# A transformer block on eight cores: first stage pipelined by x slab, a norm row loaded earlier, the MLP output's norm split, the sigmoid from Exp and Ln

## Reference

```python
hn = rms_norm(h, g_pre_mix)
u, q, k, v, f_logit = split(hn @ w_in)          # f_logit + b_f
y_pool = multiscale_pool(u, w_pool, pool_scale)
y_attn = forgetting_attention(q, k, v, log_sigmoid(f_logit))
y = concat(rms_norm(y_pool, g_pool_out), rms_norm(y_attn, g_attn_out)) @ w_out
h = h + rms_norm(y, g_post_mix)
a = relu(rms_norm(h, g_pre_mlp) @ w_up)
h = h + rms_norm((a * a) @ w_down, g_post_mlp)
gate = sigmoid(rms_norm(h, g_ple_gate) @ w_gate)
h = h + rms_norm(gate * (p @ w_ple), g_post_ple)
```

## Time and profile before

| what | us |
|---|---|
| median of 6 runs | 1717.58 |
| lowest and highest | 1696.63, 1854.65 |
| the profiled execution | 1719.45 |
| its span on core 4, the slowest | 1718.3 |
| TensorE busy in the span | 1615.6 (94%) |
| VectorE, ACT, GpSimd busy | 558.9, 504.4, 121.4 |
| read from and written to HBM | 252.16 MB, 25.17 MB |

### The profile page before, as it was taken

How to read it: one execution, slowest core, us unless ns; L and a number is a source line. 1 busy time by engine, 2 the same in 40 slices (tenths; PEclk the granted TensorE clock), 3 DMA queues, 4 the chain that set the end, 5 groups by cost and what they waited for, 6 DMA issues and landing times.

```text
span 1718.3 us, 24144 instructions; the slowest of 8 cores (1691.3 to 1718.3 us)
## 1 busy us (share of the span) xinstructions
PE 1615.6 (94%) x8588; PEld 826.0 (48%) x8700; DVE 558.9 (33%) x915; ACT 504.4 (29%) x1071; POOL 121.4 (7%) x241
## 2 busy tenths in 40 slices
PE   4799999999986999999999999999999999999895
PEld 2457566665553444444444444444444444444342
DVE  3564132222345444212112121212121121465445
ACT  3553444444542443110001100011000111355355
POOL 2002000001000001000000000000000000001000
PEclk9878889999998999999999999999999999999998
DMA  9544121315365448735353534435353536567646
GB/s 238 156 136 74 31 44 26 50 26 88 61 113 109 133 132 182 125 67 93 54 98 52 97 65 83 80 67 93 55 98 51 97 66 139 143 193 190 141 126 217
DMA packets 42308, 175.71 MB, mean 102 GB/s; under 512 B 4688, under 2 KB 4944, under 8 KB 33616
## 3 DMA queue, kind: packets, MB, share of 16 engines
q0 software_dynamic: 31824, 103.20, 36.3%
q1 hardware_dynamic: 10368, 70.96, 12.5%
HBM read 252.16 MB, written 25.17 MB: 161 GB/s over the span
## 4 chain that ended last, share of the span: by engine, by line
PE 82%; DVE 5%; ACT 4%; DMA 4%; issue 4%; DVEq 0%; ACTq 0%; POOL 0%; SPq 0%; POOLq 0%
PE pb L312 81%; DMA grow<-gb 2%; DMA wring_66<-wqkv 1%; ACT junkb L330 1%; PE pb L693 1%; DMA wring_65<-wv 1%; ACT stats L330 1%; ACT L330 0%; DVE accd L340 0%; ACT rstdB L330 0%; DVE m_115 L345 0%; DVE m_111 L345 0%; DVE m_113 L345 0%; DVE m_110 L345 0%; DVE m_114 L345 0%
## 5 line engine op out<-in xcount | busy, mean ns | idle before, releaser
L330 ACT ACTIVATE rt_101<-pb 128x512 f32<-128x512 f32 x64 | 38.2, 597 | 511.0 <-PE pb L312 510.5
L312 PE MATMUL pb<-hT,wslot_104 128*128 128x512 bf16 x512 | 111.3, 379 | 2.0 <-DVE hT L340 2.0
L312 PE MATMUL pb<-wslot_106,hidden 128*128 128x512 bf16 x504 | 111.9, 379 | 0.4
L312 PE MATMUL pb<-wslot_107,hidden 128*128 128x512 bf16 x503 | 111.8, 379 | 0.5
L312 PE MATMUL pb<-wslot_105,hidden 128*128 128x512 bf16 x497 | 110.7, 379 | 0.8
L312 PE MATMUL pb<-hT,wslot_105 128*128 128x512 bf16 x512 | 111.2, 379 | 0.0
L312 PE MATMUL pb<-hT,wslot_106 128*128 128x512 bf16 x512 | 111.2, 379 | 0.0
L312 PE MATMUL pb<-hT,wslot_107 128*128 128x512 bf16 x512 | 111.2, 379 | 0.0
L312 PE MATMUL pb<-wslot_104,hidden 128*128 128x512 bf16 x500 | 109.9, 379 | 0.6
L340 DVE TENSOR_TENSOR hidden<-rt_101 128x512 bf16<-128x512 f32 x64 | 44.3, 692 | 177.9 <-ACT rt_101 L330 177.9
L340 DVE TENSOR_TENSOR hidden<-rt_102 128x512 bf16<-128x512 f32 x64 | 44.3, 692 | 174.1 <-ACT rt_102 L330 174.1
(11 more groups left out here) (310 smaller groups left out, 2356.5 us busy)
## 6 DMA issues: line engine op xcount, KB each, us to landing
wslot_104<-wmlp POOLq DMA_DIRECT2D x32, 512.0 KB, 9.5
wslot_105<-wmlp POOLq DMA_DIRECT2D x32, 512.0 KB, 8.7
wslot_106<-wmlp POOLq DMA_DIRECT2D x32, 512.0 KB, 9.4
wslot_107<-wmlp POOLq DMA_DIRECT2D x32, 512.0 KB, 9.5
xst_59<-xT SPq DMA_DIRECT2D x6, 1024.0 KB, 5.8
xst_60<-xT SPq DMA_DIRECT2D x5, 1024.0 KB, 5.5
xst_61<-xT SPq DMA_DIRECT2D x5, 1024.0 KB, 7.3
xt_95<-xo SPq DMA_DIRECT2D x4, 1024.0 KB, 6.7
```

Source lines behind the costliest of these rows:

```text
L312: pe.op(lambda h: h.matmul(o, lhsT, rhs, start=bool(start), stop=bool(stop), skip_group_check=True), r=(lhsT, rhs), w=(o,), signal=bool(st ...
L330: act.op(lambda h: h.activation(o, i, func, **kw), r=r, w=w)
```

## The change

Four parts.

1. First stage: a slab's casts and squares are emitted ahead of the sums of the slab before, squares in one ACT pass of 2048 columns, sums in two wide adds. The casts of the next block's first slab stand ahead of this block's root, its squares behind all evictions. The queries that were in the first block go elsewhere: none after block 0, 16 after blocks 1 and 2 (eight on each side of the `onesf` matmul), 32 after block 3. SyncE waits before some x loads for quarters of the key weights, and the second query ring (`wring_68`) is issued after the second block.
2. `grow` for the mixer is loaded when the first half of `u` is done (`biasT` lies elsewhere for that); `y_pair` yields twice per tile between scaling and transposing.
3. `norm2` is split: the second half of the add goes to GpSimd (not for tile 7); `norm2h` is the cast; `norm2b`, the squares in two halves with the root and a change of sign, comes a tile later, in the middle of the next tile's `down` calls; the transposes come two tiles later, inside a `down`. The norm of tile 7 is emitted among the first gates.
4. The sigmoid is Exp(-Ln(1 + Exp(-z))), three ACT passes. `wple` is in two pieces, the scale by the last `grow` starts after the first eight gates, two per gate.

```diff
@@ startup
+        def casts(h, sl):
...
+        def squares(h, sl):
+            n = 4 * h + sl
+            actf(sq[n % 2], xst[n % 3], AF.Square)
+            if n == 1:
+                sp.wait(wk_ev[2])
+            xload(n + 3)
...
+        fills = ((), ((0, 0),), ((1, 0),), ((0, 1), (1, 1)))
+        for h, (own, half) in enumerate(halves):
             for sl in range(4):
+                if sl or not h:
+                    casts(h, sl)
+                    squares(h, sl)
+                if sl:
+                    sums(h, sl - 1)
+                project(h, sl)
+            sums(h, 3)
...
+            if fill:
+                query(fill[0][0], fill[0][1], 6, range(0, 8))
+            mm(bank(7), onesf, acc2[:, 0, :], True, True)
+            if h < 3:
+                casts(h + 1, 0)
+            rsqrt(rb, bank(7), float(D))
+            if fill:
+                query(fill[0][0], fill[0][1], 6, range(8, KC))
...
+            if h < 3:
+                squares(h + 1, 0)
+            if h == 1:
+                pool.wait(Ev(act.sem, "act", act.count, "act"))
+                pload(3)
@@ mix_main
         done.add("uA")
+        sp.dma(grow, gb_in[0])
...
         while "att" not in done:
             yield
-        sp.dma(grow, gb_in[0])
@@ y_pair
             v_ts(yb[:, i, 1024:2048], yb[:, i, 1024:2048], col1(r_a, i))
-        yield
+            yield
+            yield
@@ norm2
         v_stt(m[t], m[t], col1(r_m, t), grow, ALU.mult, ALU.mult)
-        v_tt(m[t], m[t], h1t[t], ALU.add)
+        if t < NT - 1:
+            v_tt(m[t][:, 1024:2048], m[t][:, 1024:2048], h1t[t][:, 1024:2048], ALU.add, eng=pool)
+            v_tt(m[t][:, 0:1024], m[t][:, 0:1024], h1t[t][:, 0:1024], ALU.add)
+        else:
+            v_tt(m[t], m[t], h1t[t], ALU.add)
         sp.dma(h2s[t], m[t])
+
+    def norm2h(t):
         actf(hb[:, t, :], m[t], AF.Copy)
-        actf(h1j[t], m[t], AF.Square, accum=col1(ssq_h2, t))
-        rsqrt(col1(r_3, t), col1(ssq_h2, t), float(D))
+
+    def norm2b(t):
+        for k in range(2):
+            actf(junkb.rearrange("p a n -> p (a n)"), m[t][:, k * 1024:k * 1024 + 1024], AF.Square,
+                 accum=col1(ssq_h2, 2 * t + k))
+        v_sum(col1(s_h2, t), ssq_h2[:, 2 * t:2 * t + 2])
+        rsqrt(col1(r_3, t), col1(s_h2, t), float(D))
+        v_ts(col1(r_3, t), col1(r_3, t), -1.0)
@@ last chunk of the MLP
         for q in range(1, 4):
-            down(wslot[(n + q - 1) % 4], 3, q, t)
-        norm2(t)
+            between = ()
+            if t >= 2 and q == 2:
+                between = [(k, lambda hf=hf, t=t: transpose_tile(hb[:, t - 2, :], 2, hT[:, t - 2], halves=(hf,)))
+                           for hf, k in enumerate((5, 11))]
+            down(wslot[(n + q - 1) % 4], 3, q, t, between)
+            if t and q == 2:
+                norm2b(t - 1)
+        if t < NT - 1:
+            norm2(t)
+            norm2h(t)
...
-        if t >= 1:
-            transpose_tile(hb[:, t - 1, :], 2, hT[:, t - 1])
@@ gate
-        actf(sg, bank(b), AF.Sigmoid, scale=col1(r_3, t))
+        actf(sg, bank(b), AF.Exp, scale=col1(r_3, t))
+        actf(sg, sg, AF.Ln, bias=1.0)
+        actf(sg, sg, AF.Exp, scale=-1.0)
...
-        if lag:
-            lag.pop(0)()
+        for _ in range(2):
+            if lag and "g2" in done:
+                lag.pop(0)()
@@ the first gates
-            if q == 0 and t == 4:
+            gate(wslot[(n + q) % 4], q, t)
+            if q == 0 and t == 1:
+                norm2(NT - 1)
+                sp.dma(grow, gb_in[2])
+            if q == 0 and t == 2:
+                norm2h(NT - 1)
+            if q == 0 and t == 3:
+                transpose_tile(hb[:, 6, :], 2, hT[:, 6])
+                norm2b(NT - 1)
+            if q == 0 and t == 5:
                 transpose_tile(hb[:, 7, :], 2, hT[:, 7])
-            gate(wslot[(n + q) % 4], q, t)
+            if q == 0 and t == 7:
+                done.add("g2")
```

More of the change, by code:

```diff
@@ L213, in build_nc @@
     wgate_in = din("wgate", (4, 4, 128, 4, 512))
[L214 removed]
+    wple_in = din("wple", (2, 128, 2, 1024))
     wpool_in = din("wpool", (128, 4, 2, 256))
@@ L428, in q_evac @@
         v_tt(QT[hp % 2][:, hh, half * 512:half * 512 + 512], bank(b), rstdB[:, half * 512:half * 512 + 512], ALU.mult)
+    halves = ((1, 0), (0, 0), (1, 1), (0, 1))
     def startup():
         wv, wk, wq = wring[0], wring[1], wring[2]
[L432 to L435, removed]
-            for sl in range(4):
[L437 to L467, removed]
@@ new lines, in casts @@
+        def casts(h, sl):
+            own, half = halves[h]
+            n = 4 * h + sl
+            xs = xst[n % 3]
+            for k in range(4):
+                kc = sl * 4 + k
+                o = hg(own)[:, kc, half * 512:half * 512 + 512]
+                if k % 2 == 0:
+                    v_ts(o, xs[:, k, :], gc[:, 0, kc:kc + 1])
+                else:
+                    actf(o, xs[:, k, :], AF.Copy, scale=gc[:, 0, kc:kc + 1])
+        def squares(h, sl):
+            n = 4 * h + sl
+            actf(sq[n % 2], xst[n % 3], AF.Square)
+            if n == 1:
+                sp.wait(wk_ev[2])
+            xload(n + 3)
@@ new lines, in sums, with project @@
+        def sums(h, sl):
+            q = sq[(4 * h + sl) % 2]
+            if sl == 0:
+                v_tt(acc2, q[:, 0:2, :], q[:, 2:4, :], ALU.add)
+                return
+            v_tt(q[:, 0:2, :], q[:, 0:2, :], q[:, 2:4, :], ALU.add)
+            v_tt(acc2, acc2, q[:, 0:2, :], ALU.add)
+            if sl == 3:
+                v_tt(acc2[:, 0, :], acc2[:, 0, :], acc2[:, 1, :], ALU.add)
+        def project(h, sl):
+            own, half = halves[h]
+            H, t0 = hg(own), half * 512
+            for k in range(4):
+                kc = sl * 4 + k
+                for t in range(4):
+                    mm(bank(t, 0, 264), H[:, kc, t0 + t * 128:t0 + t * 128 + 128], wv[:, kc, :],
+                       kc == 0, kc == KC - 1, last=(k == 3))
+                for hh in range(2):
+                    mm(bank(4 + hh), wk[:, kc, hh * 128:hh * 128 + 128], H[:, kc, t0:t0 + 512],
+                       kc == 0, kc == KC - 1, last=(k == 3))
@@ new lines, in query @@
+        def query(hh, half, b, kcs):
+            for kc in kcs:
+                mm(bank(b), wq[:, kc, hh * 128:hh * 128 + 128], hgo[:, kc, half * 512:half * 512 + 512],
+                   kc == 0, kc == KC - 1)
+        fills = ((), ((0, 0),), ((1, 0),), ((0, 1), (1, 1)))
+        for h, (own, half) in enumerate(halves):
+            for sl in range(4):
+                if sl or not h:
[5 more added lines that the diff above has]
+            sums(h, 3)
+            rb = rstdB[:, (1 - own) * 1024 + half * 512:(1 - own) * 1024 + half * 512 + 512]
+            fill = fills[h]
+            if fill:
[6 more added lines that the diff above has]
+                query(fill[0][0], fill[0][1], 6, range(8, KC))
@@ L479, in startup @@
                 k_evac(0, hh, own, half, 4 + hh)
-            q_evac(0, qhh, qhalf, 6)
+            if fill:
+                q_evac(0, fill[0][0], fill[0][1], 6)
+            for hh, qhalf in fill[1:]:
+                query(hh, qhalf, 7, range(KC))
+                q_evac(0, hh, qhalf, 7)
+            if h < 3:
[3 more added lines that the diff above has]
+                pload(3)
         pload(4)
@@ L685, in norm1, with transpose_tile @@
         actf(jk2, o, AF.Square, accum=col1(ssq_h1, i))
-    def transpose_tile(src, gi, dst, r=mmr):
-        for hf in range(2):
+    def transpose_tile(src, gi, dst, r=mmr, halves=(0, 1)):
+        for hf in halves:
             b = mmbank(r)
@@ L815, in build_nc, with down @@
     ssq_m = cols(NT * 4)
-    def down(w, c, q, t):
+    def down(w, c, q, t, between=()):
         b = mmbank()
@@ L820, in down @@
             mm(bank(b), hidden[:, t // 4, kc, (t % 4) * 128:(t % 4) * 128 + 128], w[:, kc, :], kc == 0, kc == KC - 1)
+            for k, fn in between:
+                if k == kc:
+                    fn()
         md = m[t][:, q * 512:q * 512 + 512]
```

36 lines of the change are left out of this document (18 added, 18 removed).

## The result

The changed kernel takes 1687.09 us (median of 10 runs), the kernel before 1717.9 (median of 20): the ratio is 0.9866, with a 95% interval from 0.9811 to 0.9921: a gain of 0.8 to 1.9%. That is 31 us by the medians, where the prediction had 21. Some runs, three of these ten, show a still lower clock on a whole die, and the ratios and the counts of runs here leave those out. The profiled execution took 1686.79, its span is 1685.8 on core 6. Which cores set the time is the first thing to read.

A forecast was written before the change was run, and what follows sets the result against it. TensorE's projections, 81% of the chain that ended last, were taken as the bound, the first stage bound first by loads. Terms: -16 - 12 + 12 - 11.4 + 8.0 - 1.3 = -20.7, giving 1697 us; range 1669 to 1722.

The forecast's parts named there:

- First block, -6: First block of the first stage: weights land at 35, block ends at 40, a gain of 6 us (2 to 10).
- First stage, the rest, -10: First stage after its first block: shorter stalls at block boundaries, a gain of 10 us (6 to 13).
- The 4 us put down there for slow slabs: First stage: 4 us lost if three rounds of the x buffers take 11 us.
- Norm row and yields, -12: Mixer's end: early norm row wins 10.3 us, yields 3.2, less 1.5 for what is late next: -12 (-6 to -16).
- Norm of the MLP output, cycle 12.0 + X: MLP output's norm: a tile's cycle goes from 12.59 to 14.3 us, last tile +12 (+4 to +29).
- X: GpSimd's half of the add in the MLP output's norm, taken as 2.3 us.
- the 11.4 off: Start of the gates: they no longer stand behind norm and hb, -11.4 us, so the first comes +0.6 in all.
- rival 2: MLP output's norm: VectorE's and GpSimd's halves of the add take turns, 8 us more, 1705 us; chance 0.16.
- Gates, +8.0: Gates: ACT sets the pace at 3.76 us a gate, 132.8 where 124.9 pass before, +8.0.
- Tail, -1.3: After the last sum: the table load that stands alone on the path, 1.28 us, goes: -1.3.
- Rivals 1 and 4: MLP output's norm: TensorE sets the pace, cycle 11.4, 1677 us, chance 0.17; GpSimd's add decides, 7.2, 1731 us, chance 0.12.
- Rival 3: First stage: bound by x slabs, 8 us won instead of 16, 1705 us; chance 0.10.

The follow-up runs named there:

- experiments 1 and 2: Kernel before with new first stage alone: 1685.44 us; changed kernel with old one: 1722.63; boundary casts late in new stage: 1693-1694 or near 1718; early in old: 1692.65.
- grow_only: Kernel before with only the mixer's norm row loaded early, when the first half of u is done; one run, 1706.84 us.
- sig_gates: Changed kernel with one Sigmoid instead of Exp, Ln and Exp in the first 16 gates; 1688.48 us.
- best: Changed kernel with previous tile's squares between root and hb, whole add on VectorE, one Sigmoid in first 16 gates, tile 6 transposed ahead of the gates; 1664.11 us.
- fill: Changed kernel with the whole add on VectorE and the previous tile's squares on ACT between the root and hb; 1661.66 us (0.9757).
- dve_add: Changed kernel with the whole add of the norm on VectorE for every tile; 1688.1 us.

## Why the prediction was right, and where it was wrong

The time came out in the range, 10 us below the point (1687 against 1697). That is luck in good part: on cores at full clock the work became 10.9 us shorter, about half of the 20.7 of the sum, and 20 us came from the pair at the lower clock, whose going no term held. The run in which a pair kept it took 1710.

- **First block, -6: measured -3.4.** The loads are where they were looked for, and the end came at 43.4 on average, not at 40. GpSimd's wait between value quarters (21.0 us in all on core 6) and the key weights behind it still decide.
- **First stage, the rest, -10: measured -7.8** on cores at full clock. The boundary came out as worked out (3.9 of waits at the first, about 2 beside queries). The stage takes 73.3 at full clock where 70 was worked out; on core 6 matmuls behind the first and third boundaries run slow (1.09 for four of 264 columns, then 0.61) and cost 3.7, where 1.5 was put for it. The working took the 0.71 to 0.8 of core 4 as a given that would cost the new stage 7 us. This is the step that failed most: the low clock is not given, it comes with the old first stage, and its absence is worth about 25 us on the slowest core. The earlier trace rows stop at 120 us, while the low clock lasts to 250; the earlier trace rows showed a slower and a faster core, and the runs of before lay in two groups, at 1697 and 1717 (experiments 1 and 2 show whose it is). The 4 us put down there for slow slabs don't follow from the 11 us a round beside them: four rounds of 11 are 2 more than 12 x 3.52. No such wait came.
- **Norm row and yields, -12: measured -17.9,** past the bound of -16. The mechanism was right; both halves were undersized. The row gives 9.7 (10.3 were in the sum, less 1.5 for what is late next), the yields, by what is left, 7.0 where 3.2 were credited. Against grow_only TensorE waits 4.3 less ahead of the transposes of yb on core 6 (8.0 for the scales of yb and the roots before them, then 3.7), and the clock of the stretch goes from 0.95 to 1.00. Another 3.6 came between 128 and 483 us, which no step had; why is open.
- **Norm of the MLP output, cycle 12.0 + X: measured 15.47.** The 12.0 fits, X was mis-sized: 2.3 was taken, it is 3.47 with its hops. Seven cycles are then 20.2 longer, not 12, and with the 11.4 off, the first gate comes 8.8 later, not 0.6. That is the mechanism of rival 2, to which the forecast gave 0.16; its time of 1705 did not come, because of the terms above. The Trainium skill's rule ("SBUF — State Buffer", section "SBUF: two separate sides") that such a pair excludes each other agrees with the rows: 3.41 beside VectorE's half, 2.35 without it. The nearest row, the copy of 128x128, gave the engine's own time well (2.4 from 0.30).
- **Gates, +8.0: measured +13.8.** To the end of the last square they take 137.2 on average where 132.8 was worked out; the rest is that cores at full clock took 123.4 before, not the 124.9 of core 4. ACT's 3.76 per gate was right to the digit, and so, nearly, was the 8.5 of tile 7's work among the gates: 1536.28 to 1573.19 less seven gates is 10.6, of which ACT waits 2.3 for TensorE. But the working let ACT alone set the pace. TensorE lost its head start there, waiting 4.9 and 2.6 us in the first gates and running at half clock for some stretches. After that TensorE is the bound again, at 3.88 a gate. Sigmoid in place of Exp, Ln and Exp gains only 1 to 2 us of it (sig_gates), so the price per gate was not what counted. That tile 7 among the gates was, is argued from the waits for its hT (5.6 in sig_gates, 8.7 in best) and not shown by a run without it.
- **Tail, -1.3: measured -1.7.** Right; ACT loads one table where it loaded 17.
- Rivals 1 and 4 fell: the cycle did not come to 11.4, and GpSimd's half is 2.35 alone, not 7.2. That ACT's order, and not TensorE, sets the cycle is shown from the other side by fill against dve_add, where the same work in another place gives 11.95 for 15.24. Rival 3 fell: in blocks 2 to 4 TensorE waits for banks, not for x.

## What to carry to other kernels

When a wait of one queue is filled with work from elsewhere, look at where that work stands relative to what starts the wait: two squares and a root ahead of it make a cycle of 15.24, the same instructions inside it one of 11.95, half a us over TensorE's own 11.4. Splitting the add of two SBUF tiles over VectorE and GpSimd gained nothing here: 3.41 us for the two halves side by side, 2.29 for the whole on VectorE. And before a gain is worked out, read the clocks of all cores, to the end of the low stretch: here the order of the first stage, most likely through one stall per block, decided how often a pair of cores lost its clock, and that was worth more than all the microseconds counted in the stage.
